# The delta rule's triangular inverse: 64-row diagonal blocks packed side by side, and products in two quadrants of the array

## The chip, the cores and the metric

One core of one Trainium2 chip runs the whole program. The metric is the device time of one execution in microseconds; the kernel before has a median of 3513.79 us over 3 runs (3511.43 to 3515.95). PE is TensorE, DVE VectorE, ACT ScalarE, POOL GpSimd, SP the engine that issues the weight loads.

## The reference, cut to what matters

The program is two blocks of two layers each on 512 tokens of width 1024. The second block's layers hold, besides two attentions and a feed-forward part, a gated delta rule with 6 heads of 64 columns, in chunks of 64 tokens (8 chunks). All of it is float32.

```python
beta = jax.nn.sigmoid(b_logit.astype(f32)).reshape(bsz, n, C, H).transpose(0, 3, 1, 2)
g = jnp.cumsum(g.reshape(bsz, n, C, H).transpose(0, 3, 1, 2), axis=-1)
...
decay = jnp.exp(jnp.where(incl, g[..., :, None] - g[..., None, :], -jnp.inf))
k_beta = k * beta[..., None]
lower = jnp.where(strict, jnp.einsum('bhncd,bhnsd->bhncs', k_beta, k) * decay, 0.0)
rhs = jnp.concatenate([v * beta[..., None], k_beta * jnp.exp(g)[..., None]], axis=-1)
sol = lax.linalg.triangular_solve(lower, rhs, left_side=True, lower=True, unit_diagonal=True)
u, w = jnp.split(sol, 2, axis=-1)
attn = jnp.einsum('bhncd,bhnsd->bhncs', q, k) * decay
```

The kernel solves the triangular system with 128 tokens at a time, so the matrix `lower` of a tile of tokens is 128x128 here, and it forms the inverse of I + lower explicitly.

## The kernel before, in words

The function `delta_inverse` (L2693) is one stage, called once in each of the two layers of the second block, so it runs twice in an execution. Ahead of it stands `transpose_tiles` "deltaT", behind it `delta_scan`, which reads the inverse as XT (six heads, each 128 rows by four tiles of 128 columns) and attnT. Stages are separated by a barrier of all engines; inside a stage each engine runs a list of instructions written out by hand, in order, and waits on semaphores.

The stage begins with a start per head, of six heads. PE spreads the cumulated gates (L2726) and makes the dots of k with k_beta and with q (L2733, contraction over 64 rows). DVE masks the gates (L2807), ACT takes the exponential into `dec` (L2789), DVE multiplies it in, which gives LT (L2816) and attnT (L2817), and cuts out of LT the entries next to the diagonal that belong to blocks of size 1, negated (L2819). POOL adds the identity to it (L2853), which is the inverse XT of blocks of size 2, and masks LT strictly (L2855). PE transposes XT (`turn_start`, L2718) and ACT keeps it as X (L2782).

The loop then doubles the size of the inverted diagonal blocks: sizes 2, 4, 8, 16, 32 and 64, each for all six heads, 36 units (size, head) in this order. A unit works on a head's four 128x128 tiles in one bank of `ps` (512 columns):

- PE: Y = first product of LT and X (L2754), four calls of 128x128x128; ACT copies it (L2800).
- PE: Z = second product of Y and XT (L2766), four calls; DVE multiplies it with the mask `high{s}` of this size into M (L2828).
- POOL adds M to XT (L2867). Up to size 32 (30 units) PE also transposes M (L2775, four calls) and DVE adds the result to X (L2838).

A call of a float32 product shows as two records in the trace, one call of `transpose` as one. In PE's list the second product of a unit stands one unit behind the first, and the transposing two units behind; Y has two buffers and M four. Side work is put between the units: on DVE the head norm of another attention's output (L2669 after unit 6, L2673 after 9, four L2677 after 11 to 14, L2690 after 18), on POOL its root (L2682, L2684 at unit 14) and four multiplications with a gain (L2861 at units 20 to 23).

Other places that the text speaks of: L457 (in `transpose_tiles`, products with the identity whose results alternate between `ps` rows 0 to 63 and 64 to 127), L903 (the same with four strips of 32 rows), L2917 (in `delta_scan`, six products of 64 output rows that alternate between the two halves of `ps`), L2894 (also there), L3037 (products of 62 columns in the compressed attention). In the rows of the trace `128*64` is rows by columns of the stationary operand, and `128x64` the moving operand. The tiles X, XT, LT, Y and M all lie in the buffer `b_work`, or `b_work2` that the rows show under the same name.

## Time and profile before

| | |
|---|---|
| median of 3 runs | 3513.79 us (3511.43 to 3515.95) |
| the profiled execution, time | 3491.05 us |
| its span (first to last instruction) | 3489.0 us |
| mean granted TensorE clock of it | 0.957 |
| PE busy | 3245.3 us, 93% |
| DVE, ACT, POOL busy | 1930.0, 1318.4, 458.6 us |
| the changed stage, first layer | about 1834.6 to 1941.4 us of the span |
| the changed stage, second layer | ends about 2943.4 us |

Busy time is the time with an instruction of the engine under way. A wait is put down to the instruction that released it. The granted clock is a share: 1.00 is 2.4 GHz, 0.50 is 1.2 GHz. PE and PEld are the two halves of TensorE's records, the product and the load of the stationary operand ahead of it; products are pipelined, so a record's duration is longer than the distance between two of them.

### The profile page before, as it was taken

The page shows a single profiled execution, that of the slowest core. Times are in us where ns is not written, and L with a number is a line of the kernel's source. Part 1 is how long each engine was busy: PE and PEld are TensorE (multiplying, and loading weights), DVE is VectorE, ACT ScalarE, POOL GpSimd, SP SyncE. Part 2 cuts the span into 40 slices and gives each one's busy share as a digit, 9 for nine tenths or more (in the row PEclk, how much of TensorE's full clock was granted, in tenths as well). Part 3 has the DMA queues.
Part 4 walks back from the last instruction along what each step waited for, and adds up shares of the span by engine and source line. Part 5 has one row for each costly group of instructions (what it writes and reads, how often), then busy time and mean ns, then how long its engine had stood idle before and what let it go on. Part 6 is the DMA issues. An engine that isn't in the chain of part 4 may idle for free. (4 is left out here: it accounts for less than half of the span.)

```text
span 3489.0 us, 44598 instructions
## 1 busy us (share of the span) xinstructions
PE 3245.3 (93%) x16768; PEld 2703.2 (77%) x16768; DVE 1930.0 (55%) x3616; ACT 1318.4 (38%) x2748; POOL 458.6 (13%) x390
## 2 busy tenths in 40 slices
PE   8998999999989999699989899999798989899996
PEld 6777788878767888588769878887687679788885
DVE  4776434337764434265576466564473855474754
ACT  4454423234453323243353333234332542332324
POOL 1031000010210000003026302020030046010010
PEclk9999999999999999899799999999897999999998
DMA  4111222131102222132000123221221000223221
GB/s 160 60 41 49 85 97 93 65 108 59 55 13 88 96 95 97 58 111 68 25 1 1 49 76 99 91 97 61 101 94 47 1 1 1 76 91 100 97 93 46
DMA packets 37325, 239.54 MB, mean 69 GB/s; under 512 B 4464, under 2 KB 5232, under 8 KB 14960
## 3 DMA queue, kind: packets, MB, share of 16 engines
q1 hardware_dynamic: 36528, 234.51, 19.8%
q8 instruction: 138, 2.26, 0.3%
q10 hardware_dynamic: 576, 2.10, 0.2%
q14 instruction: 83, 0.68, 0.1%
HBM read 234.49 MB, written 2.10 MB: 68 GB/s over the span
## 5 line engine op out<-in xcount | busy, mean ns | idle before, releaser
L260 PE MATMUL ps<-b_hl,bff_whl 128*128 128x512 f32 x704 | 275.6, 392 | 2.8 <-DVE b_hl L619 2.8
L261 PE MATMUL ps<-b_hl,bff_whl 128*128 128x512 f32 x704 | 275.1, 391 | 0.0
L262 PE MATMUL ps<-b_hl,bff_whl 128*128 128x512 f32 x704 | 274.9, 390 | 0.0
L243 DVE SCALAR_TENSOR_TENSOR bff_whl<-ring,b_cols,bff_whl 128x512 fp32r<-128x512 f32 (+1 forms) x224 | 153.2, 745 | 203.2 <-ACT bff_whl L230 202.9
L240 DVE TENSOR_TENSOR aff_whl<-ring,aff_whl 128x512 fp32r<-128x512 f32 x160 | 99.8, 686 | 223.6 <-ACT aff_whl L228 223.6
L230 ACT ACTIVATE bff_whl<-ring,b_cols 128x512 fp32r<-128x512 f32 (+1 forms) x224 | 136.6, 681 | 182.1 <-PE ps L262 182.1
L261 PE MATMUL ps<-aff_whl,a_u 128*128 128x512 f32 x512 | 204.3, 399 | 0.0
L260 PE MATMUL ps<-a_hl,aff_whl 128*128 128x512 f32 x512 | 201.1, 393 | 2.8 <-DVE a_hl L619 2.8
L260 PE MATMUL ps<-aff_whl,a_u 128*128 128x512 f32 x512 | 201.7, 394 | 0.0
L260 PE MATMUL ps<-ain_whl,a_hl 128*128 128x512 f32 (+3 forms) x512 | 190.1, 371 | 11.9 <-DVE a_hl L619 7.2
L262 PE MATMUL ps<-aff_whl,a_u 128*128 128x512 f32 x512 | 200.7, 392 | 0.0
L262 PE MATMUL ps<-a_hl,aff_whl 128*128 128x512 f32 x512 | 200.4, 391 | 0.0
L261 PE MATMUL ps<-a_hl,aff_whl 128*128 128x512 f32 x512 | 200.4, 391 | 0.0
L228 ACT CAST aff_whl<-ring 128x512 fp32r<-128x512 f32 x160 | 87.5, 620 | 276.4 <-PE ps L262 272.5
L261 PE MATMUL ps<-ain_whl,a_hl 128*128 128x512 f32 (+3 forms) x512 | 187.2, 366 | 0.0
L262 PE MATMUL ps<-ain_whl,a_hl 128*128 128x512 f32 (+3 forms) x512 | 186.9, 365 | 0.0
L240 DVE TENSOR_TENSOR bff_whl<-ring,bff_whl 128x512 fp32r<-128x512 f32 x128 | 84.7, 720 | 147.8 <-ACT bff_whl L228 147.8
L243 DVE SCALAR_TENSOR_TENSOR aff_whl<-ring,a_gains,aff_whl 128x512 fp32r<-128x512 f32 x128 | 87.6, 747 | 125.7 <-ACT aff_whl L230 125.5
L260 PEld LDWEIGHTS ps<-b_hl,bff_whl 128*128 128x128 f32 x704 | 132.9, 189 | 31.2 <-DVE b_hl L619 3.6
L262 PEld LDWEIGHTS ps<-b_hl,bff_whl 128*128 128x128 f32 x704 | 133.0, 189 | 27.7
L261 PEld LDWEIGHTS ps<-b_hl,bff_whl 128*128 128x128 f32 x704 | 133.0, 189 | 27.7
L228 ACT CAST bff_whl<-ring 128x512 fp32r<-128x512 f32 x128 | 70.3, 619 | 212.8 <-PE ps L262 205.2
(498 smaller groups left out, 8003.8 us busy)
## 6 DMA issues: line engine op xcount, KB each, us to landing
ring<-in_a_w_ff SPq DMA_DIRECT2D x64, 1024.0 KB, 4.8
ring<-in_b_w_up SPq DMA_DIRECT2D x32, 1024.0 KB, 4.9
ring<-in_a_w_in SPq DMA_DIRECT2D x16, 1024.0 KB, 5.4
ring<-in_b_w_down SPq DMA_DIRECT2D x16, 1024.0 KB, 4.8
ring<-in_b_w_in_att SPq DMA_DIRECT2D x12, 1024.0 KB, 4.9
ring<-in_b_w_up SPq DMA_DIRECT2D x16, 768.0 KB, 4.2
ring<-in_b_w_in_conv SPq DMA_DIRECT2D x12, 768.0 KB, 4.3
ring<-in_a_w_out SPq DMA_DIRECT2D x8, 1024.0 KB, 5.0
```

The costliest lines, as they stand in the source:

```text
L228: self.c.nc.scalar.copy(self.part(j, 0, k), src[:, k, :]).then_inc(self.hi_made, 1)
L230: self.c.nc.scalar.activation(self.part(j, 0, k), src[:, k, :], ACT.Copy, scale=g[:, row + k:row + k + 1]).then_inc(self.hi_made, 1)
L240: self.c.nc.vector.tensor_tensor(self.part(j, 1, k), src[:, k, :], self.part(j, 0, k).bitcast(F32), ALU.subtract).then_inc(self.lo_made, 1)
L243: self.c.nc.vector.scalar_tensor_tensor(out=self.part(j, 1, k), in0=src[:, k, :], scalar=g[:, row + k:row + k + 1], in1=self.part(j, 0, k) ...
L260: nc.tensor.matmul(bank, sh, mh, start=start, stop=False)
L261: nc.tensor.matmul(bank, sh, ml, start=False, stop=False)
L262: return nc.tensor.matmul(bank, sl, mh, start=False, stop=stop)
```

## The change

The 128x128 matrix of a tile is block diagonal in two 64x64 blocks up to size 32, and the change keeps only these: X, XT, Y and M of a head are 128 rows by four tiles of 64 columns, the low 64 rows holding the low block and the high 64 rows the high block. A product is then eight calls of 64x64x64 (four tiles, two blocks), the low block in rows and columns 0 to 63 of the array, the high block in 64 to 127. The transposing becomes such a product with the identity. At size 64 only one 64x64 corner is computed: Y in the quadrant from low rows to high `ps` rows, Z from high to low. ACT copies the two blocks of XT into the 128-column tiles `whole` in these six units, DVE writes the negated corner there, and POOL clears the other corner at the start of the stage and has no addition at size 64. POOL's strict mask of LT goes. The second product stands two units behind the first, the transposing four; Y has four buffers and M eight. The constants lose 576 columns.

```diff
-def delta_inverse(c, name, g, kT, kbT, qT, LT, attnT, dec, X, XT, Y, M, norm_of, z4, z_gain):
+def delta_inverse(c, name, g, kT, kbT, qT, LT, attnT, dec, X, XT, whole, Y, M, norm_of, z4, z_gain):
...
+    W = TT * HD
+    low, high = slice(0, HD), slice(HD, P)
+    halves = (low, high)
+    ps = lambda bank, t, r: c.ps[r, bank, t * HD:(t + 1) * HD]
+    tile = lambda a, t, r: a[r, t * HD:(t + 1) * HD]
+    LT4, whole4 = (a.rearrange("p h (t n) -> p h t n", t=TT) for a in (LT, whole))
...
+            def turn(bank, src):
+                for t in range(TT):
+                    for r in halves:
+                        ins = nc.tensor.matmul(ps(bank, t, r), tile(src, t, r), c.ident[r, r], start=True, stop=True)
+                return ins
+
...
-                for t in range(TT):
-                    ins = nc.tensor.transpose(c.ps[:, 6 + h % 2, sl[t]], XT[:, h, sl[t]], c.ident)
-                ins.then_inc(turned, 1)
+                turn(6 + h % 2, XT[:, h, :]).then_inc(turned, 1)
...
-            for i in range(U + 2):
+            for i in range(U + 4):
...
                         pe.wait_ge(X_kept, i + 1)
-                        pe.wait_ge(strict, i + 1)
...
-                        ins = nc.tensor.matmul(c.ps[:, i % 2, sl[t]], LT[:, h, sl[t]], X[:, h, sl[t]],
-                                               start=True, stop=True)
+                        if s < HD:
+                            for r in halves:
+                                ins = nc.tensor.matmul(ps(i % 2, t, r), LT4[r, h, t, r], tile(X[:, h, :], t, r),
+                                                       start=True, stop=True)
+                        else:
+                            ins = nc.tensor.matmul(ps(i % 2, t, high), LT4[low, h, t, high], tile(X[:, h, :], t, low),
+                                                   start=True, stop=True)
                     ins.then_inc(Ys, 1)
-                u = i - 1
+                u = i - 2
...
-                        ins = nc.tensor.matmul(c.ps[:, 2 + u % 2, sl[t]], Y[:, u % 2, sl[t]],
-                                               XT[:, h, sl[t]], start=True, stop=True)
+                        if s < HD:
+                            for r in halves:
+                                ins = nc.tensor.matmul(ps(2 + u % 2, t, r), tile(Y[:, u % 4, :], t, r),
+                                                       tile(XT[:, h, :], t, r), start=True, stop=True)
+                        else:
+                            ins = nc.tensor.matmul(ps(2 + u % 2, t, low), tile(Y[:, u % 4, :], t, high),
+                                                   tile(XT[:, h, :], t, high), start=True, stop=True)
                     ins.then_inc(Zs, 1)
-                m = i - 2
+                m = i - 4
...
-                    for t in range(TT):
-                        ins = nc.tensor.transpose(c.ps[:, 4 + m % 2, sl[t]], M[:, m % 4, sl[t]], c.ident)
-                    ins.then_inc(M_turned, 1)
+                    turn(4 + m % 2, M[:, m % 8, :]).then_inc(M_turned, 1)
```

The lists of ACT, DVE and POOL, the constants and the call:

```diff
-                nc.scalar.copy(X[:, h, :], c.banks(6 + h % 2)).then_inc(X_kept, 1)
+                nc.scalar.copy(X[:, h, :], c.ps[:, 6 + h % 2, 0:W]).then_inc(X_kept, 1)
...
-            for i in range(U):
+            for i, (s, h) in enumerate(units):
                 act.wait_ge(Ys, i + 1)
-                if i >= 2:
-                    act.wait_ge(Zs, i - 1)
-                nc.scalar.copy(Y[:, i % 2, :], c.banks(i % 2)).then_inc(Y_kept, 1)
+                if i >= 4:
+                    act.wait_ge(Zs, i - 3)
+                r = slice(0, P) if s < HD else high
+                nc.scalar.copy(Y[r, i % 4, :], c.ps[r, i % 2, 0:W]).then_inc(Y_kept, 1)
+                if s == HD:
+                    act.wait_ge(XT_grown, i - H + 1)
+                    for r in halves:
+                        nc.scalar.copy(whole4[r, h, :, r], by4(XT[r, h, :]))
...
-                nc.vector.tensor_tensor(by4(XT[:, h, :]), by4(LT[:, h, :]), four(c.cst("high1")), ALU.mult
-                                        ).then_inc(cut, 1)
+                for r in halves:
+                    ins = nc.vector.tensor_tensor(by4(XT[r, h, :]), LT4[r, h, :, r],
+                                                  c.cst("high1")[r].unsqueeze(1).broadcast_to([HD, TT, HD]), ALU.mult)
+                ins.then_inc(cut, 1)
             for i in range(U + 2):
                 if i < U:
-                    s = units[i][0]
+                    s, h = units[i]
                     dve.wait_ge(Zs, i + 1)
-                    if i >= 4:
-                        dve.wait_ge(XT_grown, i - 3)
-                        dve.wait_ge(M_turned, min(i - 3, both))
-                    nc.vector.tensor_tensor(by4(M[:, i % 4, :]), by4(c.banks(2 + i % 2)), four(c.cst(f"high{s}")),
-                                            ALU.mult).then_inc(masked, 1)
+                    if s == HD:
+                        nc.vector.tensor_scalar(whole4[low, h, :, high], by4(c.ps[low, 2 + i % 2, 0:W]), -1.0, None,
+                                                ALU.mult).then_inc(masked, 1)
+                    else:
+                        if i >= 8:
+                            dve.wait_ge(XT_grown, i - 7)
+                            dve.wait_ge(M_turned, i - 7)
+                        nc.vector.tensor_tensor(by4(M[:, i % 8, :]), by4(c.ps[:, 2 + i % 2, 0:W]),
+                                                c.cst(f"high{s}").unsqueeze(1).broadcast_to([P, TT, HD]), ALU.mult
+                                                ).then_inc(masked, 1)
...
-                    nc.vector.tensor_tensor(X[:, h, :], X[:, h, :], c.banks(4 + m % 2), ALU.add).then_inc(X_grown, 1)
+                    nc.vector.tensor_tensor(X[:, h, :], X[:, h, :], c.ps[:, 4 + m % 2, 0:W], ALU.add
+                                            ).then_inc(X_grown, 1)
...
+            nc.gpsimd.memset(whole4[high, :, :, low], 0.0).then_inc(cleared, 1)
+            pool.wait_ge(cleared, 1)
             for h in range(H):
                 xt = by4(XT[:, h, :])
                 pool.wait_ge(cut, h + 1)
-                nc.gpsimd.tensor_tensor(xt, xt, four(c.ident), ALU.add).then_inc(started, 1)
-                L = by4(LT[:, h, :])
-                nc.gpsimd.tensor_tensor(L, L, four(c.cst("strict01")), ALU.mult).then_inc(strict, 1)
+                nc.gpsimd.tensor_tensor(xt, xt, c.cst("ident64").unsqueeze(1).broadcast_to([P, TT, HD]), ALU.add
+                                        ).then_inc(started, 1)
...
+                if s == HD:
+                    continue
...
-                nc.gpsimd.tensor_tensor(XT[:, h, :], XT[:, h, :], M[:, i % 4, :], ALU.add).then_inc(XT_grown, 1)
+                nc.gpsimd.tensor_tensor(XT[:, h, :], XT[:, h, :], M[:, i % 8, :], ALU.add).then_inc(XT_grown, 1)
...
-    cols["strict01"] = (lane[:, None] < lane[None, :]) * 1.0
...
-    for s in (1, 2, 4, 8, 16, 32, 64):
...
-        same = (lane[:, None] // (2 * s)) == (lane[None, :] // (2 * s))
-        low = same & ((lane[:, None] // s) % 2 == 1) & ((lane[None, :] // s) % 2 == 0)
-        cols[f"high{s}"] = -1.0 * low.T
+    here, there = lane[:, None] % HD, np.arange(HD)[None, :]
+    cols["ident64"] = (here == there) * 1.0
+    for s in (1, 2, 4, 8, 16, 32):
+        same = here // (2 * s) == there // (2 * s)
+        cols[f"high{s}"] = -1.0 * (same & (here // s % 2 == 0) & (there // s % 2 == 1))
...
-        LT, attnT, X, XT = (work[:, 6 * i:6 * i + 6, :] for i in range(4))
+        LT, attnT, XT = (work[:, 6 * i:6 * i + 6, :] for i in (0, 1, 3))
+        packed = lambda a, n: a.rearrange("p a s -> p (a s)").rearrange("p (a n) -> p a n", a=n)
+        half_X, half_XT = packed(work[:, 12:15, :], GDN_H), packed(work[:, 15:18, :], GDN_H)
...
-            delta_inverse(c, "dinv", g, kT, kbT, qT, LT, attnT, dec, X, XT, hT[:, 0:2, :], hT[:, 2:6, :],
+            delta_inverse(c, "dinv", g, kT, kbT, qT, LT, attnT, dec, half_X, half_XT, XT,
+                          packed(hT[:, 0:2, :], 4), packed(hT[:, 2:6, :], 8),
```

## Rows read from the trace of the kernel before

**Rows 1.** Header of the profile page.

```profile
span 3489.0 us, 44598 instructions
```

**Rows 2.** Table of stretches: from:to, length, busy (x instructions) of five engines, PEclk, DMA share, GB/s.

```profile
1866.00:1938.00 72.00, 71.89 (x645) 71.57 (x644) 47.89 (x70) 19.32 (x33) 48.35 (x39) 1.00 0.01 1
```

**Rows 3.** Groups by form, 1859.5 to 1941.6 us: shapes, xcount, busy us, mean ns, idle before.

```profile
L2867 POOL TENSOR_TENSOR b_work<-b_work 128x512 f32<-128x512 f32 x36 | 45.7, 1273 | 28.7 <-DVE b_work L2828 28.5
L2754 PE MATMUL ps<-b_work 128*128 128x128 f32 x288 | 39.0, 281 | 0.0
...
L2828 DVE TENSOR_TENSOR b_work<-ps,const_b 128x512 f32<-128x512 f32 x36 | 24.8, 689 | 32.9 <-PE ps L2766 32.6
...
L2775 PE MATMUL ps<-const_b,b_work 128*128 128x128 f32 x120 | 18.1, 273 | 0.1
...
L2677 DVE TENSOR_TENSOR b_mix<-b_mix,b_rows 128x256 f32<-128x256 f32 x4 | 3.8, 939 | 0.0
...
L2690 DVE TENSOR_TENSOR b_mix<-b_mix,b_sbssq 128x1024 f32<-128x1024 f32 x1 | 1.9, 1919 | 0.0
...
L2673 DVE TENSOR_REDUCE b_sbssq<-b_sbsq 128x16 f32<-128x1024 f32 x1 | 1.2, 1211 | 0.0
```

**Rows 4.** Timeline of PE around one unit: start us, length us, engine, line, xrecords.

```profile
1890.06 0.60 PE L2775 MATMUL ps<-const_b,b_work 128*128 128x128 f32 x4
...
1890.50 1.06 PE L2754 MATMUL ps<-b_work 128*128 128x128 f32 x8
...
1892.72 1.06 PE L2754 MATMUL ps<-b_work 128*128 128x128 f32 x8
```

**Rows 5.** Timeline of PE in three other stages, records on part of the array.

```profile
1947.44 0.57 PE L2917 MATMUL ps<-b_work,b_kel 128*64 128x64 f32 x12 [0.72 <-DVE b_work L2975]
...
1643.00 7.21 PE L457 MATMUL ps<-const_b,b_proj 128*64 128x128 f32 x128
...
48.37 1.08 PE L903 MATMUL ps<-const_a,a_mix 128*32 128x128 f32 x32
```

**Rows 6.** The instructions of L2917: duration ns min/median/max.

```profile
L2917 PE MATMUL ps<-b_work,b_kel x72: 222/222/270, 1947.4 to 2961.7; 128*64 128x64 f32 x72
```

**Rows 7.** Table of stretches, columns as in rows 2: L457, and the compressed attention (L3037).

```profile
1643.70:1650.50 6.80, 6.80 (x123) 6.63 (x120) 3.86 (x6) 2.63 (x6) 1.69 (x2) 1.00 0.01 2
...
1657.00:1684.00 27.00, 21.24 (x120) 20.59 (x120) 8.41 (x15) 2.55 (x4) 0.00 (x0) 0.51 0.23 78
```

**Rows 8.** Groups by form, whole span and first layer: 128x256 tiles, and L3037.

```profile
L3114 DVE TENSOR_TENSOR b_mix<-ps,cmpst 128x256 f32<-128x256 f32 x12 | 5.1, 425 | 17.8 <-PE ps L3063 17.8
...
L2342 ACT COPY nsapT<-ps 128x256 f32<-128x256 f32 x24 | 8.7, 362 | 0.0
...
L2394 POOL TENSOR_TENSOR a_proj<-a_proj,a_g_ret 128x256 f32<-128x256 f32 x8 | 5.6, 721 | 10.3 <-POOLq L150 10.3
...
L3037 PE MATMUL ps<-b_blocks,ring 128*128 128x62 f32 x64 | 13.9, 421 | 5.3 <-DVE b_blocks L3087 5.3
```

**Rows 9.** Timeline: the last head's start, the loop's begin and its last two adds.

```profile
1855.77 0.69 DVE L2819 TENSOR_TENSOR b_work<-b_work,const_b 128x512 f32<-128x512 f32 x1
...
1857.55 1.25 POOL L2853 TENSOR_TENSOR b_work<-b_work,const_b 128x512 f32<-128x512 f32 x1
...
1858.85 0.72 PEld L2718 LDWEIGHTS ps<-const_b,b_work 128*128 128x128 f32 x4 [2.50 <-POOL b_work L2853]
...
1859.77 3.08 PE L2754 MATMUL ps<-b_work 128*128 128x128 f32 x16
...
1938.88 2.48 POOL L2867 TENSOR_TENSOR b_work<-b_work 128x512 f32<-128x512 f32 x2 [0.52 <-DVE b_work L2828]
```

**Rows 10.** Waits, 1834 to 1860 us: who waited for whom, us in total, times, longest.

```profile
POOL b_work L2853 <- DVE b_work L2819: 11.3, 5, 8.2
```

**Rows 11.** Group of a clearing on POOL, whole span.

```profile
L3525 POOL MEMSET b_ksT<- 64x1024 f32 x2 | 1.9, 950 | 50.7 <-POOLq L150 50.7
```

**Rows 12.** DMA issues: xcount, KB each, median us from issue to landing.

```profile
const_b<-in_const_b SPq DMA_DIRECT2D x1, 1196.0 KB, 5.0
```

More of the change, by code:

```diff
@@ L2703, in delta_inverse @@
     by4 = lambda a: a.rearrange("p (t n) -> p t n", t=TT)
-    with c.stage(name, "rows", "row_masked", "decays", "dots", "decayed", "LT_made", "strict", "cut", "started", "turned",
+    W = TT * HD
[4 more added lines that the diff above has]
+    LT4, whole4 = (a.rearrange("p h (t n) -> p h t n", t=TT) for a in (LT, whole))
+    with c.stage(name, "rows", "row_masked", "decays", "dots", "decayed", "LT_made", "cleared", "cut", "started", "turned",
                  "X_kept", "Ys", "Y_kept", "Zs", "masked", "XT_grown", "M_turned", "X_grown", "squared", "summed",
                  "powered") as (
-            block, rows, row_masked, decays, dots, decayed, LT_made, strict, cut, started, turned, X_kept, Ys, Y_kept,
+            block, rows, row_masked, decays, dots, decayed, LT_made, cleared, cut, started, turned, X_kept, Ys, Y_kept,
             Zs, masked, XT_grown, M_turned, X_grown, *norm_sems):
```

## Prediction, made before the changed kernel was run

> **What bounds the kernel now.** I read the header of the page, then the table of stretches, then the groups of the changed loop, then the timeline of one of its turns. The profiled execution has a span of 3489.0 us [rows 1] and took 3491.05 us as a run; the median of the runs is 3513.79 us, 22.7 us (0.6%) above it. I make the sum against the profiled execution and move the difference over to the median.
>
> The changed function runs twice, once in each layer of the second block. In a stretch inside its loop over 36 units PE is busy 71.89 of 72.0 us at a granted clock of 1.00 [rows 2]: DVE (47.9), ACT (19.3) and POOL (48.4) have room. So a unit costs what PE's queue costs. Per unit PE works off 8 records for the first product, 8 for the second (four calls of fp32, two records each) and 4 for the turn of M. In the timeline the turn's four records last 0.60 us, the eight of a product 1.06 us, and the next unit's first product begins 2.22 us after this one's [rows 4]. With the 0.275 us that one record takes from start to end [rows 3], records follow each other every (1.06 - 0.275) / 7 = 0.112 us. Check: 16 x 0.112 + 4 x 0.109 = 2.23 us. The loop of a layer issues 36 x 16 + 30 x 4 = 696 records, 77.5 us, and lasts from 1859.77 (the first product) to 1941.36 us (the end of POOL's last add, 1938.88 + 2.48) [rows 9]: 81.6 us, so 4.1 us are its start at half clock, the first hand-overs and its tail.
>
> **What the change does to PE's work.** Up to size 32 each product is eight calls of 64x64x64, alternating between the low and the high diagonal quadrant, so 16 records; the turn is no transpose any more but eight products with the identity, 16 records also. That is 48 records instead of 20 per unit for 30 units, 1440 in all. At size 64 it is 8 + 8 records, all of a product in one quadrant, for 6 units: 96.
>
> The price of a record decides everything, and no 64-row, 64-column product on two diagonal quadrants is in this trace. The nearest row is L2917: 64 weight columns, 64 moving columns, calls alternating between the two column halves. Its twelve records last 0.57 us [rows 5] with 0.222 us for one [rows 6]: (0.57 - 0.222) / 11 = 0.032 us between starts, the slower first ones in it. L457, alternating in the same way with 128 moving columns, keeps (7.21 - 0.273) / 127 = 0.0546 us over 128 records, and L903 with four column strips (1.08 - 0.273) / 31 = 0.026 us over 32 [rows 5] (0.273 is L2775's [rows 3]). Both are a stream of 128 columns every 0.109 us in each part of the array, L2775's spacing, and the parts at the same time; with 64 columns L457's would be 0.027. I take 0.029 us, between that and L2917's 0.032, and 0.058 for a record whose neighbour uses the same quadrant. The bounds are 0.026 us below and 0.058 us above (no overlap at all). That it holds for long is not shown: the longest run below 0.05 us is L903's 32 records, and the new loop wants it for 1440.
>
> So a unit up to size 32 is 48 x 0.029 = 1.39 us for 2.23 before, and a unit of size 64 is 16 x 0.058 = 0.93 us for 1.79. PE's sum is 1440 x 0.029 + 96 x 0.058 = 41.8 + 5.6 = 47.3 us.
>
> **What comes late next.** The tiles of the other engines halve to 256 columns. DVE has a 128x256 form from ps at 0.425 us, ACT's copy is 0.362, POOL's add 0.721 [rows 8], for 0.689 (DVE) and 1.273 (POOL) at 512 columns [rows 3]. Per unit DVE then has 0.85 us, POOL 0.72, ACT 0.36, all under PE's 1.39. The round trip of a head is no bound: two products and a turn (3 x 0.47), three ends (3 x 0.22), copy, mask and add (1.2) and about 0.6 for the hand-overs make 3.9 us, and the head comes round only after 6 units, 8.3 us. The diff also puts Z two units behind Y and the turn four behind, with Y in four and M in eight buffers, so each hand-over has a unit or more.
>
> What is exposed is DVE's side work. The norm's steps between the units (L2690 at 1.919 and the square of the same width, L2673 1.211, four of L2677 at 0.939 [rows 3]: 8.8 us) fitted before into the 0.86 us that DVE had free per unit. Now it has 0.54 free, and an add has about half a unit of slack: 0.9 + 0.2 + 0.9 + 0.9, some 2.9 us of stall. POOL's own side work has five units of slack, as the sum of XT is needed only in the head's next Z: nothing.
>
> At size 64 ACT gets two copies of 64x256 into the whole tile per unit: 0.36 + 2 x 0.39 = 1.14 us against PE's 0.93. I put down 1.0 us for it. XT_grown, on which they wait, is six units old. DVE writes the corner of size 64 straight into the whole tile, so POOL's last adds (they end 2.48 us after 1938.88 [rows 9]) are gone: the tail shrinks by about 1.7 us. The start of the loop at half clock and the first waits stay. So 4.1 us of overhead become about 3.0, and the loop is 47.3 + 3.0 + 2.9 + 1.0 = 54.2 us: 27.4 less.
>
> **The start of the stage.** POOL loses the strict mask (1.27 us per head) and its identity add halves. PE waited 2.5 us in front of the last start's turn, because POOL began the add of head 5 at 1857.55 although DVE's cut ended at 1856.46 [rows 9]. Now the cut is two instructions of 64 rows (some 0.85 us in all for 0.69), then 0.72 on POOL: the turn can start at about 1857.4 instead of 1858.85, so 1.5 us less. The other heads' starts are hidden behind the dots. The turns of the starts cost PE 16 x 0.029 = 0.46 for 0.44 us: nothing. The memset of 64x1536 (1.4 us after the 0.950 of 64x1024 [rows 11]) lies in POOL's first wait of 8.2 us [rows 10]: nothing; without that wait it would cost 1.4. The constant table loses 576 columns, 288 of 1196 KB that landed in 5.0 us [rows 12]: at most 1.2 us, once; I take 0.6. The scan reads XT whole as before.
>
> **Sum:** 2 x (27.4 + 1.5) + 0.6 = 58.4 us. 3491.05 - 58.4 = 3432.6 for the profiled execution, and 3513.8 - 58.4 = 3455 for the median.
>
> **The clock, row and rule.** In the table of stretches PE is busy 21.24 of 27.0 us at 0.51, with L3037's products of 62 moving columns [rows 8], so small products can be busy and still stay at 1.2 GHz; but L457, which loads 64 of the array's columns, is at 1.00, 2.4 GHz, throughout [rows 7]. Work on part of the array has thus kept the full level here, and the loop's records leave no more room between them than L457's do. I keep full clock. The Trainium skill speaks against the change at another place: its page TensorE: Matmul & The Clock Gate, in "Wait - 56ns, not 53.3ns?", says that where the firmware decodes, each MATMUL costs some 62 ns of sequencer time, which binds small products. By that page the estimate would be 1536 x 0.062 = 95 us of PE per layer and a kernel about 30 us slower. The trace doesn't agree for short stretches (26 ns for 32 records) nor for long ones down to 55 ns, and is silent on long ones below that. The page TensorEngine Tiling (Array Packing), "Key Properties", says that tiles work independently of each other, which L2917 agrees with.
>
> **The rivals.**
> (a) *DVE is next.* Its side work, 8.8 us, is exposed whole, and it may lengthen beside POOL's work (L2677 takes 0.939 us for 256 columns, L3114 0.425 [rows 3, 8]). For it: DVE is 0.85 + side work of a 1.39 us unit. Against it: the deeper buffers. Loop 47.3 + 3 + 8.8 + 3 = 62.1: saves 19.5 + 1.5 per layer, 42 us, so 3472; with records at 0.035 besides, 3489. Chance 0.15.
> (b) *PE's instruction queue can't be filled so fast* (slower). PE has to be given 48 weight loads and 48 matmuls per unit instead of 20 and 20. For it: every run below 0.05 us per record is short and could have been queued while PE waited; the longest sustained is L457's 0.0546. Against it: no row shows a slower limit. At 0.0546 the layer is 1536 x 0.0546 + 3 = 86.9 us for 81.6: 3.8 slower after the start's gain, 7.6 in all, 3521. It turns at (81.6 + 1.5 - 3 - 5.6) / 1440 = 0.052 us per record. Chance 0.09. (This is the mechanism of the rule from the Trainium skill above; by its figure the time would be 3544.)
> (c) *The diagonal quadrants don't overlap, or the clock stays at 1.2 GHz* (slower). Either gives about 0.058 us per record: 83.5 + 5.6 + 3 = 92.1, 9 us per layer slower, 3532. For it: the stretch at 0.51; no row has both halves of rows and columns split. Against it: L2917, L457, L903. Chance 0.08.
> (d) *Nothing moves*, a mix of (a) and (b) near 0.05 us. Chance 0.04.
> The forecast has 0.64.
>
> **How the numbers follow.** A measurement here can tell from no change about 0.2%, 7 us. The forecast's own range: 0.026 instead of 0.029 gives 2 x 4.3 less, no stalls of DVE 2 x 2.9 less: 3441; some stalls more: 3468. Rival (a) reaches 3489. So 3441 to 3490 leaves out (b), (c) and (d), 0.21 with what is lost at the edges; (d) sits just above. Faster: 0.64 + 0.15 and nothing of the rest, less a little: 0.79; same 0.05; slower 0.16.
>
> **What would show it.** Right: in the loop, 16 records of a product last some 0.65 us (15 x 0.029 + 0.22), first products of neighbouring units start 1.4 us apart, the loop takes 52 to 57 us, the clock is 1.00, ACT's copy 0.36, DVE's mask 0.43; PE's wait ahead of the last start's turn is about 1 us. (a): idle time of PE that DVE's X or mask ends, with starts 0.03 apart. (b): the same spacing of 0.05 or more in the low and the high quadrant together, at clock 1.00, with idle time put down to issue or to nothing. (c): 0.058 within a quadrant and never two at once, or PEclk near 0.5. The forecast is wrong if a unit takes over 1.9 us.

## The result, and the profile after

The changed kernel has a median of 3467.57 us over 4 executions (3456.17 to 3468.62); the kernel before, taken beside it, 3514.87 over 4 (3511.43 to 3533.16). The ratio is 0.9863, with a 95% interval of 0.9821 to 0.9905: 33 to 63 us faster, 47 by the medians. The forecast was 3455, with a range of 3441 to 3490; it is right in sign and range, and 13 us too low.

The profiled execution of the changed kernel took 3468.37 us. First the header of its page, then from the tables of stretches (columns as in rows 2) the two start parts and two pieces of the loop:

```profile
span 3466.6 us, 48222 instructions
```

```profile
1860.50:1897.50 37.00, 36.61 (x223) 33.72 (x224) 16.35 (x30) 8.70 (x29) 4.33 (x6) 0.50 0.00 0
...
1900.00:1940.00 40.00, 38.08 (x1261) 37.21 (x1258) 27.20 (x59) 9.90 (x27) 25.79 (x33) 1.00 0.02 5
2847.00:2870.00 23.00, 20.95 (x222) 19.09 (x221) 16.86 (x30) 8.70 (x29) 5.04 (x7) 1.00 0.01 2
2873.00:2913.00 40.00, 39.31 (x1309) 38.94 (x1306) 27.41 (x60) 10.45 (x29) 26.23 (x33) 0.99 0.02 4
```

The loop runs at the full clock in both layers, and PE is still its bound (against [rows 2]): 38.1 and 39.3 of 40 us busy, DVE 27, POOL 26, ACT 10. What sticks out is the first row: the start part of the first layer, wide products for the most part, runs at a granted clock of 0.50, that is 1.2 GHz, for all of its 37 us, with PE busy nearly throughout. The same work in the second layer has 1.00 and is over in 24 us.

The timeline of PE (start, length, records) in the second layer's loop, which answers to [rows 4]:

```profile
2876.48 0.63 PE L2765 MATMUL ps<-b_work 64*64 64x64 f32 x16
2876.95 0.63 PE L2782 MATMUL ps<-b_work 64*64 64x64 f32 x16
2877.41 0.63 PE L2722 MATMUL ps<-const_b,b_work 64*64 64x64 f32 x16
2877.88 0.63 PE L2765 MATMUL ps<-b_work 64*64 64x64 f32 x16
```

One unit follows the other after 2877.88 - 2876.48 = 1.40 us, for 2.22 before, and 48 records in it make 0.0292 us each. The groups by form of that loop (2870.7 to 2921.7 us), which answer to [rows 3, 8]:

```profile
L2900 POOL TENSOR_TENSOR b_work<-b_work 128x256 f32<-128x256 f32 x30 | 21.6, 729 | 17.7 <-DVE b_work L2856 17.5
...
L2856 DVE TENSOR_TENSOR b_work<-ps,const_b 128x256 f32<-128x256 f32 x30 | 12.6, 421 | 15.3 <-PE ps L2782 15.2
L2867 DVE TENSOR_TENSOR b_work<-b_work,ps 128x256 f32<-128x256 f32 x30 | 12.6, 419 | 1.8 <-PE ps L2722 1.0
L2818 ACT COPY b_work<-ps 128x256 f32<-128x256 f32 x30 | 11.2, 372 | 30.2 <-PE ps L2765 30.2
L2822 ACT COPY b_work<-b_work 64x256 f32<-64x256 f32 x12 | 4.8, 403 | 0.2
...
L2677 DVE TENSOR_TENSOR b_mix<-b_mix,b_rows 128x256 f32<-128x256 f32 x4 | 2.6, 650 | 0.0
L2850 DVE TENSOR_SCALAR b_work<-ps 64x256 f32<-64x256 f32 x6 | 2.5, 416 | 1.8 <-PE ps L2785 1.6
...
L2690 DVE TENSOR_TENSOR b_mix<-b_mix,b_sbssq 128x1024 f32<-128x1024 f32 x1 | 1.5, 1508 | 0.0
```

DVE and ACT wait for PE, and POOL for DVE, not the other way round. The halved tiles cost what rows 8 said, and the norm's steps became cheaper than before (0.650 for 0.939 us, 1.508 for 1.919).

Now the span, piece by piece. A stage is cut here at its first product, at the first Y of the loop, and at the scan's first product; "low" is the time in it at the half clock, which is 1.2 GHz, and "outside" is all of the span that is not these two stages. The last two rows are repetitions that the experiments below describe.

| us | start part 1 (low) | loop 1 | start part 2 (low) | loop 2 | outside (low) | span |
|---|---|---|---|---|---|---|
| before | 25.1 (1.0) | 81.9 | 25.1 (1.6) | 83.3 | 3273.5 (292) | 3489.0 |
| after | 39.1 (37.5) | 51.0 | 24.2 (0.0) | 50.9 | 3301.4 (367) | 3466.6 |
| before, again | 25.1 (1.0) | 82.0 | 35.8 (24.0) | 82.4 | 3280.4 (309) | 3505.7 |
| after, third | 24.6 (1.1) | 51.9 | 24.3 (0.2) | 53.5 | 3268.2 (281) | 3422.5 |

The two profiled spans differ by 22.4 us only. The loops gave 30.9 + 32.4 = 63.3 us, 8.5 more than forecast. The first start part took 14.0 back, the second gave 0.9, and 27.9 us were lost outside, in work that the change doesn't touch. That last loss goes with the clock: the column "low" outside is 75 us longer. So the profiled execution of before was one at a high mean clock (0.957), and the one of after at 0.941.

The record has the mean clock of every execution, so that executions at one clock can be compared. Those of the changed kernel (this run and the two repetitions below) and those of the kernel before (59, beside the experiments) give:

| mean clock | changed kernel, us | kernel before, us |
|---|---|---|
| 0.941 | 3468.4, 3472.8 | 3529.0 |
| 0.951 | 3441.0, 3444.3 | 3500.3 to 3508.9 (6) |
| 0.958 | 3424.2 | 3485.0 to 3489.6 (6) |

At one clock the change is worth some 63 us (straight lines through all executions give 3445.9 and 3508.9 at 0.950, and none lies more than 6 us off its line). The medians lie closer together because the clock is not alike: its median is 0.943 over the changed kernel's 14 executions and 0.950 over the 59.

### The profile page after: what moved, and what is told of

Its sections match the earlier page's. It is cut to its first block and busy times, and to the rows that moved or that the text cites. A ratio compares the mean times of both kernels' runs of the same rounds, so it can differ in the third digit from the quotient of the medians.

```text
span 3466.6 us, 48222 instructions
## 1 busy us (share of the span) xinstructions
PE 3234.7 (93%) x18592; PEld 2682.1 (77%) x18592; DVE 1899.0 (55%) x3628; ACT 1309.6 (38%) x2772; POOL 390.9 (11%) x368
```

## The experiments

Theory at the start: the loop is PE's, at 0.029 us a record; what is missing of the forecast is clock. Its rivals: DVE's side work stalls PE; the change makes the clock fall; the instruction stream cannot be delivered.

**Both kernels again.** No edit.

> The changed kernel once more, unedited, timed against the one before. If the unit of 1.40 us in the loop is the whole story, both layers save 28 to 34 us and the kernel is 58 to 66 us faster (ratio near 0.982). If the low clock in the first layer's start (37 us at half clock in the first profile) belongs to the change, it shows again in this profile and the ratio stays near 0.986; if it is a matter of chance, other places are low this time and the start may run at full clock (24 us instead of 39).

> The kernel before, unedited, as a kernel of its own: what its runs differ by among themselves and at which granted clock. If the 22 us between its profiled execution and its median are the clock, runs near 3491 us have about 0.957 and runs near 3514 us about 0.94 to 0.95, and the ratio is 1.00.

After, again: 3467.84 us (3441.01 to 3472.79, 6 executions), ratio 0.9877 (0.9829 to 0.9925). Before, again: 3507.6 (3486.23 to 3531.02, 10). The gain holds. The loops repeat to 0.3 us in the changed kernel (50.7 and 51.0, for 51.0 and 50.9) and to 0.9 us in the one before (82.0 and 82.4, for 81.9 and 83.3). The start parts do not: in this run of after both are low, 39.1 us with 37.5 low; in that of before the second is low for 24.0 us and takes 35.8. From the tables of stretches, the first layer's start part of after, again, and the second layer's of before, again:

```profile
1847.00:1885.50 38.50, 38.11 (x236) 35.10 (x236) 16.86 (x30) 8.70 (x29) 5.37 (x7) 0.52 0.00 1
```

```profile
2843.00:2878.70 35.70, 32.34 (x167) 29.63 (x168) 15.48 (x24) 9.66 (x29) 14.53 (x12) 0.67 0.00 1
```

So a start part at the half clock is no property of the changed kernel alone. It costs 39.1 - 24.2 = 14.9 us there and 35.8 - 25.1 = 10.7 in the kernel before, whose clock came back before the loop. In these low start parts, and in the three of the variants below that have no idle stage ahead, the clock fell 1.6 to 1.9 us after the stage's first product, which itself came after 1.7 us without a product; the start parts at the full clock begin after the same 1.7 us.

**The norm behind the loop.** DVE's norm steps move out from between the units (POOL's power with them):

```diff
-                if i == 6:
-                    norm.square(dve)
-                if i == 9:
-                    norm.total(dve)
-                if 11 <= i < 11 + TT:
-                    norm.weigh(dve, i - 11)
-                if i == 18:
-                    norm.scale(dve)
+            norm.square(dve)
+            norm.total(dve)
+            for t in range(TT):
+                norm.weigh(dve, t)
+            norm.scale(dve)
```

> The head norm's steps (8.8 us on DVE, 3.2 us on POOL per layer) stand behind the loop instead of between its units; everything is still computed. Theory A, of the prediction: the gaps in the row of 1.40 us units come from DVE's side work; then they vanish, the loop's first to last Y shrinks by 2 to 3 us, and the stage is longer by some 9 us (12 of tail less 3). Theory B: the gaps belong to PE's own instruction stream (they come every 124 records); then they stay, at the same records, 0.3 to 0.7 us each, and the stage is longer by the whole 12 us. Kernel: A +18 us, B +24 us against the changed kernel.

3470.15 us (3463.04 to 3482.02, 4), ratio 0.9899: 2.6 us above the changed kernel, where both theories wanted 18 or more. The loop's records, first to last, take 50.7 and 49.7 us, for 50.0 and 49.9 in the changed kernel; the norm now stands alone behind them, and the loop part is 58.9 and 57.9, 7 to 8 us longer. That the time hardly shows it goes with the clock: in the profiled executions of this run and of after, each with one low start part, the two stages take 180.1 and 165.2 us, but all the rest 3289.1 and 3301.4. Taking DVE's side work away thus frees no time of PE. The stalls are still there. PE's weight loads in the changed kernel (timeline, first layer):

```profile
1929.12 0.54 PEld L2782 LDWEIGHTS ps<-b_work 64*64 64x64 f32 x16 [0.54 <-issue]
...
1932.38 0.48 PEld L2722 LDWEIGHTS ps<-const_b,b_work 64*64 64x64 f32 x13
1933.47 0.19 PEld L2722 LDWEIGHTS ps<-const_b,b_work 64*64 64x64 f32 x3 [0.61 <-issue]
```

The second gap falls in the middle of a group of 16, where nothing is waited for, and the profile names "issue" and no engine. Counting records from the loop's first, which is number 0, starts lie over 0.15 us apart behind records 479, 603, 727, 851, 975, 1099 and 1223 in the first layer: 124 apart, 0.28 to 0.74 us long. In the run with the norm behind the loop they fall behind the same numbers (479, 603, 727, ..., 1223). A gap that keeps its place in the instruction stream when DVE's work is taken away is not DVE's. (With the idle stage of the later runs, whose barrier comes ahead in PE's list, the gaps fall one record earlier.) The waits of PE's loads in that run's second layer say so too (who waited for whom, us in total, times, longest):

```profile
PEld ps L2782 <- issue: 1.1, 3, 0.5
PEld ps L2722 <- issue: 0.5, 1, 0.5
PEld ps L2765 <- issue: 0.4, 2, 0.2
PEld ps L2785 <- ACT b_work L2818: 0.2, 1, 0.2
```

124 records are 248 loads and products. In the loop (2870 to 2922 us) the queue that brings instructions moves 12 packets of 0.20 MB together, some 16 KB each, one per 4 us; in 72 us of the loop before it is 5:

```profile
q8 instruction: 12, 0.20, 1.5%
```

```profile
q8 instruction: 5, 0.08, 0.5%
```

The Trainium skill (Perfetto Trace Analysis, "The 4-stage abstract model") gives an instruction 64 bytes, so a packet would be 256 of them: 248 and some that only wait. The spacing of the gaps agrees. So do the packets' times: in the nine profiled executions of the changed kernel and its variants that alternate the quadrants, there are 147 gaps at such places, and in each PE's next product starts 1.2 to 1.7 us after the end of a packet of this queue. In the run with one quadrant first, below, the records at these places from 355 on start 2.5 us or more after it, and there is no gap. So PE stands still there until its next instructions have been brought.

**Shorter lags.** Z goes one unit behind Y for two, the turn two behind for four, on PE's list alone:

```diff
-            for i in range(U + 4):
+            for i in range(U + 2):
...
-                u = i - 2
+                u = i - 1
...
-                m = i - 4
+                m = i - 2
```

> Second product one unit behind the first and the turn two units behind, as before the change; the rings of four and eight buffers stay. Theory: at 1.40 us a unit has no room for the way from Y over ACT's copy back to Z (0.22 + 0.37 us and two hand-overs against 0.47 us of other work), so every unit waits some 0.3 us and PE's unit becomes 1.7 to 1.8 us: 10 to 13 us per layer, kernel +20 to +26 us against the changed one. Rival: PE's queue is filled so slowly that the waits hide behind it; then +0 to 5 us.

3444.32 us (3439.79 to 3454.49, 4), ratio 0.9826. The loops take 53.8 and 53.3 us, 2.4 to 2.8 more than the 51 of the changed kernel; I had looked for several times as much. PE's waits for ACT come up (0.9 us in the second layer for L2818 ahead of L2785, for 0.2), but most of the gaps are still "issue". The deeper pipeline is worth at most some 5 us in the two layers: against the changed kernel's third run, whose loops sum to 105.4 us, it is 1.7. That the median is 23 us better all the same does not come from the stage: its profiled execution has one low start part as that of after has, and 170.4 us in the two stages for 165.2, but outside 294 us low and 3272.1 us for 367 and 3301.4.

**One quadrant first, then the other.** In each product and turn, the loops over tiles and over halves change places:

```diff
-                for t in range(TT):
-                    for r in halves:
+                for r in halves:
+                    for t in range(TT):
```

> In each group of 16 products of 64x64 the eight of the low quadrant are issued first and then the eight of the high one, instead of taking turns; nothing else changes. In the changed kernel a pair of products starts every 58 ns, and at size 64, where one quadrant works alone, a product also starts every 58 ns, so the two quadrants run side by side. Theory 1 (only neighbours in the instruction stream overlap): 16 products take 16 x 0.058 = 0.93 us instead of 0.46, a unit goes from 1.40 to about 2.8 us, the loop from 51 to about 93 us and the kernel to about 3550 us. Theory 2 (PE looks further ahead or a product costs 29 ns wherever it stands): no change, 3468 us, loop 51.

3468.07 us (3448.58 to 3487.45, 10), ratio 0.9898. By the median it can't be told from the changed kernel, as theory 2 has it; its profiled execution took 3448.58 us with both start parts at the full clock (25.2 us each). The loop, though, has neither theory's number: the loops take 59.8 and 58.4 us, the records first to last 58.8 and 57.4, 0.036 us each for 0.029. With the neighbours alone overlapping it would have been 0.05 or more. The timeline of PE (second layer) shows why:

```profile
2860.12 0.27 PE L2765 MATMUL ps<-b_work 64*64 64x64 f32 x1
2860.17 0.22 PE L2722 MATMUL ps<-const_b,b_work 64*64 64x64 f32 x1
2860.22 0.22 PE L2765 MATMUL ps<-b_work 64*64 64x64 f32 x1
2860.23 0.22 PE L2722 MATMUL ps<-const_b,b_work 64*64 64x64 f32 x1
2860.28 0.22 PE L2765 MATMUL ps<-b_work 64*64 64x64 f32 x1
2860.29 0.22 PE L2722 MATMUL ps<-const_b,b_work 64*64 64x64 f32 x1
```

L2765 stands behind all of L2722's group in the list, and yet its first products start before the last ones of L2722: PE starts products of a free quadrant ahead of earlier ones of the busy quadrant. Three pairs overlap at each of the two changes of quadrant in a group of 16; 10 slots of 0.057 us make 0.57 us, 0.036 per record. The order in the diff, each call beside its partner, is worth 7.5 to 8.8 us per layer, and the overlap of the two quadrants is what the kernel lives on. One more thing: at 0.036 us per record there is no gap of 0.17 us or more up to record 1500. At this pace the instructions arrive in time.

**Idle time ahead of the stage.** A stage in which POOL alone clears a tile eight times (some 8 us from the first to the last) is put in front of `delta_inverse`, in both kernels:

```diff
+            with c.stage("idle", "idled") as (block, idled):
+                @block.gpsimd
+                def _(pool):
+                    for i in range(8):
+                        if i:
+                            pool.wait_ge(idled, i)
+                        nc.gpsimd.memset(sq, 0.0).then_inc(idled, 1)
```

> The kernel before, with a stage ahead of the inverse in which GpSimd alone works (eight memsets of a 128x1536 tile, some 10 to 15 us) and PE idles, in both layers. It makes the start part of the inverse begin at the low clock. Theory 1 (the clock is what separates start parts of 25 and 36 or 39 us; the kernel before recovers by itself after some 24 us): start part about 36 us in both layers with about 24 us low, loop 82 unchanged; kernel 3515 + 2 x 12 of idling + about 15 = 3555 us. Theory 2 (the low clock is not set by the idle time ahead): start part 25 us in at least one layer, kernel about 3539.

> The changed kernel with the same idle stage ahead of the inverse in both layers. Theory 1 (a start part that begins at the low clock stays there to its end in the changed kernel, since its 64x64 turns and the waits at them leave PE less busy than the 128-wide turns did): start part about 39 us with 37.5 us low in both layers, loop 51, kernel about 3468 + 24 + up to 15 = 3500. Theory 2 (how long the clock stays low is a matter of where the start falls, alike in both kernels): start parts between 35 and 39 us in both kernels, the low stretches of this run and of the kernel before with the same idle stage alike.

Before with it: 3544.86 us (3538.65 to 3553.1, 4). After with it: 3476.05 (3466.4 to 3497.78, 10), ratio 0.9916 to the kernel before without it. Every one of the four start parts began at the half clock. The stretches of before's two, then of after's two:

```profile
1856.00:1892.50 36.50, 33.19 (x167) 30.34 (x167) 15.48 (x24) 9.67 (x29) 14.83 (x12) 0.64 0.00 1
2873.00:2909.50 36.50, 33.19 (x166) 30.34 (x167) 15.47 (x24) 9.67 (x29) 14.67 (x12) 0.64 0.00 0
```

```profile
1846.30:1886.50 40.20, 39.81 (x236) 36.70 (x238) 16.86 (x30) 8.72 (x29) 5.65 (x7) 0.50 0.00 1
2837.60:2873.50 35.90, 33.63 (x230) 30.79 (x232) 16.86 (x30) 8.72 (x29) 5.68 (x7) 0.64 0.00 1
```

The start parts took 37.2 and 37.2 us before, 40.5 and 36.2 after. The last of these is the one that matters: the changed kernel's clock can come back inside the start part (26.0 us low of 36.2). So the theory that it never does is out. With the idle stage the two kernels are 69 us apart by the medians; without it the changed kernel's three runs are 47, 43 and 62 us from the kernel before beside them. In the profiled executions 238.4 - 179.7 = 58.7 us are in the two stages: where both kernels begin low, the gain is nearly the 61 us that it is where both begin at the full clock.

**The turns of the starts last.** PE does all decay and dot products, then the six turns; ACT copies after its last Exp. In the changed kernel, twice; in the changed kernel with the idle stage; and in the kernel before:

```diff
-                if h >= 3:
-                    turn_start(h - 3)
-            for h in range(H - 3, H):
+            for h in range(H):
                 turn_start(h)
```

> The changed kernel with the turns of the six starts taken out from between the heads' decay and dot products: PE does all gcum and dot products first, then the six turns of 16 products of 64x64, and ScalarE copies them after its last Exp. Theory 1 (the turns between the wide products are what keeps the clock low to the end of the start part): a start part that begins low has the full clock back after about 24 us, so 33 to 36 us instead of 39, and one that begins at the full clock takes about 25 to 26 us (one or two us more for the turns that stand alone); kernel 3460 to 3470. Theory 2 (the turns do not matter to the clock): a start part that begins low stays so for its whole length, 39 to 41 us; kernel 3468 to 3473.

> e9 once more, to see whether its gain over the changed kernel holds. Theory 1 (with the turns last the start part takes about 23 us and is seldom low): kernel 3434 to 3450 us, both start parts under 26 us. Theory 2 (e9's 3439 was a run of lucky clock phases): median 3455 to 3470, a start part of 35 us or more in one layer.

> The changed kernel with the turns of the starts after all wide products (as in e9) and with the idle stage of e6 and e7 ahead of the inverse, in both layers. With this idling the kernel before was low for 30.7 us from about its start part's beginning in both layers, the changed kernel for 47.8 and 30.7 us. Theory 1 (the 64x64 turns between the wide products stretch a low stretch, and without them it ends as soon as in the kernel before): low stretches of about 24 to 31 us in both layers, start parts of 34 to 36 us. Theory 2 (turns do not matter; how long it lasts is decided by where the start falls): a low stretch over 34 us, start part 38 to 40 us, in at least one layer.

> The kernel before with its turns of the starts moved behind all heads' decay and dot products; nothing else. If the turns' place matters only where they are 64x64 (theory 1), the kernel before stays at 3511 us within 0.3 per cent, start parts 24 to 26 us at the full clock and 34 to 36 where it begins low. If any turn between the wide products costs (theory 2), it gains as e9 did: 3490 to 3500 us.

The first time it took 3439.13 us (3433.71 to 3450.52, 4), ratio 0.9821, with both start parts at the full clock in 23.0 us; the time is below what either theory had. The second time 3448.8 (3433.23 to 3478.48, 6), ratio 0.984, with a first start part of 37.3 us, 34.1 low. With the idle stage 3487.12 (3475.03 to 3494.63, 10), start parts of 38.9 and 39.3 us, low nearly throughout:

```profile
1867.00:1905.50 38.50, 38.36 (x226) 35.59 (x227) 16.87 (x30) 8.41 (x29) 5.71 (x7) 0.51 0.00 1
2858.90:2898.00 39.10, 39.10 (x236) 36.41 (x237) 16.87 (x30) 8.60 (x29) 5.67 (x7) 0.50 0.00 1
```

So the 64x64 turns between the wide products do not hold the clock down: without them it stayed low as long. What the edit does give, at the full clock, is 24.2 - 23.0 = 1.2 us per layer. In the kernel before (3505.28, 3487.61 to 3536.06, 10, ratio 0.9995) it gives 25.1 - 24.2 = 0.9 us, and the time cannot be told from no change.

**The changed kernel a third time,** beside the last three. No edit.

> The changed kernel a third time, beside e11. Theory 1 (its start part often begins low and then takes 39 us): at least one start part of 39 us, median 3460 to 3472. Theory 2 (phases alone, alike for all variants): as likely as not both start parts at 24 us, median 3440 to 3455.

3446.6 us (3424.24 to 3463.15, 4), ratio 0.9836 (0.978 to 0.9891), and both start parts at the full clock:

```profile
1834.70:1859.20 24.50, 22.23 (x240) 20.37 (x242) 16.86 (x30) 8.70 (x29) 5.65 (x7) 0.98 0.01 2
1859.30:1911.00 51.70, 48.85 (x1540) 47.64 (x1537) 33.10 (x73) 18.25 (x49) 28.41 (x36) 0.98 0.02 4
2800.10:2824.30 24.20, 21.93 (x240) 20.08 (x242) 16.87 (x30) 8.70 (x29) 5.66 (x7) 1.00 0.01 2
```

This is the pair to compare, as its low time outside (281 us) is close to before's (292). 3489.0 - 3422.5 = 66.5 us: 30.0 + 29.8 from the loops, 0.5 + 0.8 from the start parts, 5.3 from outside. The same kernel thus gave medians of 3467.6, 3467.8 and 3446.6 us; with the turns last it gave 3439.1 and 3448.8. These differences are larger than the 2.4 us that the turns are worth, and they go with the mean clock: 0.942, 0.943 and 0.950, and 0.951 and 0.950. Over its 14 executions the changed kernel's median is 3466.6, over the 23 of the kernel before beside this run 3508.9.

The time outside against the low time in it, over six profiled executions (after third, e11, before, after again, e9, after): 281, 287, 292, 326, 333, 367 us low; 3268.2, 3272.7, 3273.5, 3284.8, 3289.3, 3301.4 us long. That is (3301.4 - 3268.2) / (367 - 281) = 0.39 us per us, nearly on a line, and the other five profiled executions without the idle stage lie within 4 us of it. What looked like a loss of 27.9 us outside is this.

## Why the prediction was right, and where its terms were off

**The price of a record** (taken as 0.029 from L2917, L457 and L903): right, 0.0292, and it holds for 30 units on end and not only for 32 records. That it is right to 1% is in part luck: the rows gave 0.027 and 0.032, and 0.029 was a choice between them. A unit takes 1.40 us for 1.39. Size 64 was put at 0.058; the records of one quadrant do follow each other every 0.058 us there.

**The full clock in the loop:** right. In the changed kernel the loops have 0.97 to 1.00, and what is low of them is within the first 3.4 us.

**Side work of DVE, 2.9 us of stall:** the step that failed, though its size was near, which is luck. The gaps over 0.17 us add up to 2.2 to 5.0 us per loop above the normal spacing; all but some 0.3 to 0.6 us of it belongs to the instruction stream, as their places in the run with the norm behind the loop and the ends of the packets show. This is rival (b) in small: PE's instructions can't quite be brought at 0.029 us a record, and can at 0.036. As its price I had put a pace of 0.0546 us throughout. In its place came one gap of 0.2 to 0.8 us every 124 records. The rule of the Trainium skill that I set beside it (TensorE: Matmul & The Clock Gate, "Wait - 56ns, not 53.3ns?", 62 ns of firmware per MATMUL) does not bind here: 1440 records at 29 ns.

**The copies of size 64, 1.0 us, and the overhead, 3.0:** together too much. PE waited 0.2 us for ACT at size 64. The loop came to 50.7 to 53.5 us for 54.2, and saved 29.8 to 32.4 for 27.4. Rival (a) is out: without DVE's side work the loop was no shorter.

**The start, 1.5 us less per layer:** half right at best: 0.5 to 0.9. I had the last cut end only 0.16 us later than its end in the kernel before, which is 1856.46 - 1834.6 = 21.9 us after the stage's begin. The timeline of DVE, POOL and PE's loads in the second layer, which begins at 2846.5:

```profile
2868.51 0.85 DVE L2842 TENSOR_TENSOR b_work<-b_work,const_b 64x256 f32<-64x256 f32 x2
...
2869.44 0.72 POOL L2885 TENSOR_TENSOR b_work<-b_work,const_b 128x256 f32<-128x256 f32 x1 [1.48 <-DVE b_work L2842]
...
2870.22 0.54 PEld L2722 LDWEIGHTS ps<-const_b,b_work 64*64 64x64 f32 x16 [1.66 <-POOL b_work L2885]
```

The last cut ends 22.9 us after the begin, 1.0 later. DVE works back to back there with two cuts of 64 rows for one of 128 per head (0.85 for 0.69 us), and a head with a narrow turn in it costs PE 3.68 us for 3.56 and 3.46: the "nothing" for the turns of the starts was 0.1 to 0.2 us each. POOL is no longer late, it waits for DVE, and PE's wait ahead of the last turn is 1.66 us, for 2.50 before and for about 1 that I had named as a sign.

**What the sum left out** is the clock of the start part. I had priced only what the change does to it at the full clock. Over all profiled executions, a start part was at the half clock for 24 us or more in 1 of 6 of the kernel before and its variant, in 6 of 16 of the changed kernel and its variants, and in all 6 with the idle stage. In the changed kernel one that stays low to its end costs 14.9 us, more than the 12.6 us between forecast and result. How much of the 12.6 us is start parts can't be told, as a median has no trace; that it is the clock can: at one mean clock the kernels are 63 us apart for the 58.4 of the sum, and the changed kernel's executions had 0.943 for 0.950. The rest of the difference between executions lies outside the stage. The rows of the 10 us ahead of the stage, in the execution of after, first layer and second:

```profile
1848.80:1858.80 10.00, 7.94 (x48) 7.50 (x49) 9.62 (x8) 3.59 (x6) 6.99 (x3) 0.76 0.01 2
...
2836.50:2846.50 10.00, 7.47 (x48) 6.87 (x49) 9.62 (x8) 3.59 (x6) 6.99 (x3) 0.82 0.01 2
```

The work is the same in both, and in both kernels: PE is busy 7.5 to 7.9 of 10 us, and in both kernels the mean clock is 0.76 ahead of the start parts that are low and 0.82 to 0.86 ahead of the others. Once a start part followed at 0.50, once at 1.00.

**On the profiled execution** I had forecast 3491.05 - 58.4 = 3432.6 us. Against an execution of after with as much low time outside (the third, 3424.2), the forecast is 8 us too high: the loops gave 5 us more, outside 5.3, the starts and the table 2 to 3 less. Against the one at the lower clock (3468.4) it is 36 too low. The range had no term for either.

**Open:** whether the change makes a low start part more likely (6 of 16 against 1 of 6 can be chance) and why the changed kernel's 14 executions have the lower clock by the median, which its variants had in part (0.945 with the norm behind the loop, 0.948 with one quadrant first, 0.950 and 0.951 with the turns last, 0.951 with shorter lags), and why a low stretch lasts longer in it. Nine of its ten low start parts were low for 34 to 41 us and one for 26.0; the three of the kernel before for 24.0, 26.9 and 27.0. Where the turns stand is not the cause (e10).

## What to carry to other kernels

Two quadrants of the array do give small fp32 products twice the pace for tens of microseconds, if calls of the two alternate in the list; the prices of a record from short stretches of other stages, 0.027 and 0.032, bounded the one that came. A sum made at one clock needs a term for the clock of every stage it touches, and two executions are compared only after the low time of each has been taken from the trace: here a gain of some 61 us in the two stages read as 22 in one pair of profiles. When PE idles and "issue" is named, count the records from gap to gap, and look at the instruction queue's packets, before blaming an engine.

## What the runs showed of the hardware that I had not expected

- A stream of 64x64 loads and products at 0.029 us a record has gaps of 0.2 to 0.8 us every 124 records, in which PE waits for no engine; at 0.036 us a record it has none. The instruction queue then brings 16 KB per 4 us, and each gap ends 1.2 to 1.7 us after the end of such a packet.
- A stage of wide products with PE busy 36.6 of 37.0 us stayed at 1.2 GHz for 37.5 us, in a kernel that ran the same work at 2.4 GHz in the other layer. In the turns-last kernel with the idle stage, heads of 24 records of 128 columns follow each other every 5.71 us in it, for 3.07 us at the full clock.
- Products start out of the order of the list where their quadrant is free. The Trainium skill (TensorE: Matmul & The Clock Gate, "The mechanism") has matmuls strictly in order of the program in start and end; in the run with one quadrant first, the starts of L2765 and L2722 above don't agree with that.
- The norm's step L2677 (128x256 on DVE), whose own shape is unchanged, fell from 0.939 to 0.650 us by the mean. It is slow where POOL's add runs beside it: in the kernel before the first three of a layer overlap that add (L2867, 1.27 us) for 0.83 us and take 1.11, the fourth does not and takes 0.41. In the changed kernel the overlap is 0.42 to 0.47 us and they take 0.70 to 0.75. With the norm behind the loop no add of POOL is beside them, and all eight take 0.41 to 0.43. L2690 does the same: 1.92, 1.51 and 1.22 us. From the kernel before:

```profile
1893.72 1.11 DVE L2677 TENSOR_TENSOR b_mix<-b_mix,b_rows 128x256 f32<-128x256 f32 x1
...
1895.95 0.41 DVE L2677 TENSOR_TENSOR b_mix<-b_mix,b_rows 128x256 f32<-128x256 f32 x1
```
